# Third gate and up of the first expert loaded ahead of the short expert's, and returned rows loaded and added at the end, in a two-layer decoder trunk on one Trainium2 core

## The reference, cut to what matters

```python
def moe_swiglu(h, w_router, w_gate, w_up, w_down):
    t = h.reshape(B * S, D)
    logits = (t @ w_router).astype(jnp.float32)
    top_vals, top_idx = lax.top_k(logits, TOP_K)            # 2 of 8
    top_w = jax.nn.softmax(top_vals, axis=-1)
    gates = jnp.sum(jax.nn.one_hot(top_idx, N_EXPERTS) * top_w[..., None], axis=1)
    out = jnp.zeros_like(t)
    for e in range(N_EXPERTS):
        out = out + swiglu(t, w_gate[e], w_up[e], w_down[e]) * gates[:, e:e + 1]
    return out
# x = x + moe_swiglu(rms_norm(x)); return rms_norm(x, final_norm_g)
```

## Time and profile before

| | us |
|---|---|
| median of 3 runs | 1373.53 (1372.58 to 1374.31) |
| the profiled execution, its own time | 1372.62 |
| its span, first to last instruction | 1370.8 |
| PE busy | 1327.7 (97%) |
| DVE busy | 787.6 (57%) |
| ACT busy | 658.8 (48%) |
| POOL busy | 41.1 (3%) |
| first short expert's matmul begins | 558.6 |

### The profile page before, as it was taken

The page is one execution under the profiler, slowest core; times in us unless marked ns, Lnnn a source line. Parts: engine busy times, 40 slices in busy tenths (PEclk is TensorE's granted clock), DMA queues, the critical chain, the costliest instruction groups (busy, mean ns, idle before and its releaser), DMA issues.

```text
span 1370.8 us, 16922 instructions
## 1 busy us (share of the span) xinstructions
PE 1327.7 (97%) x6365; PEld 947.2 (69%) x6365; DVE 787.6 (57%) x912; ACT 658.8 (48%) x823; POOL 41.1 (3%) x45
## 2 busy tenths in 40 slices
PE   9999999999999999999999999899998999989997
PEld 8888788888888878755666556566555666646562
DVE  6556355555569757855565466464445565545561
ACT  5444445443464756554554455454445455444451
POOL 1000001000000010100000000000000000000000
PEclk9999999999999999999999999999999999999999
DMA  9745545555456437999999999999999999999994
GB/s 385 297 158 177 183 170 184 184 185 184 157 187 226 168 121 304 390 423 426 411 427 428 429 426 427 413 427 428 426 427 427 414 427 426 427 428 428 427 427 170
DMA packets 40448, 451.63 MB, mean 329 GB/s; under 512 B 4873, under 2 KB 5001, under 8 KB 8368
## 3 DMA queue, kind: packets, MB, share of 16 engines
q1 hardware_dynamic: 37408, 440.82, 79.0%
q0 software_dynamic: 2816, 9.63, 1.8%
q10 hardware_dynamic: 144, 0.09, 0.0%
HBM read 445.52 MB, written 6.55 MB: 330 GB/s over the span
## 4 chain that ended last, share of the span: by engine, by line
PE 79%; DMA 15%; DVE 3%; ACT 1%; issue 1%; POOL 0%; SPq 0%; DVEq 0%; ACTq 0%
PE psum L1939 18%; PE psum L1941 18%; PE psum L1940 18%; PE psum L2327 16%; DMA raw<-in_moe_w_gu 8%; DMA raw_more<-in_moe_w_gu 7%; PE psum L1985 1%; PE psum L1987 1%; PE psum L1986 1%; PE psum L1995 1%; DVE w_lo L1356 1%; ACT w_hi L993 1%; PE psum L2365 1%; PE psum L2358 1%; PE psum L2017 1%
## 5 line engine op out<-in xcount | busy, mean ns | idle before, releaser
L1356 DVE TENSOR_TENSOR w_lo<-raw,w_hi 128x1024 fp32r<-128x1024 f32 (+1 forms) x152 | 267.3, 1771 | 214.4 <-ACT w_hi L993 213.4
L993 ACT CAST w_hi<-raw 128x1024 fp32r<-128x1024 f32 (+1 forms) x152 | 225.3, 1492 | 226.2 <-PE psum L1941 150.2
L1941 PE MATMUL psum<-w_hi,actA_lo 128*128 128x512 f32 (+1 forms) x752 | 292.2, 389 | 0.0
L1939 PE MATMUL psum<-w_hi,actA_hi 128*128 128x512 f32 (+1 forms) x644 | 258.1, 401 | 25.2 <-DVE w_lo L1356 24.0
L1940 PE MATMUL psum<-w_lo,actA_hi 128*128 128x512 f32 (+1 forms) x644 | 250.0, 388 | 0.0
L1939 PEld LDWEIGHTS psum<-w_hi,actA_hi 128*128 128x128 f32 x644 | 122.2, 190 | 70.2 <-DVE w_lo L1356 35.8
L1941 PEld LDWEIGHTS psum<-w_hi,actA_lo 128*128 128x128 f32 x752 | 142.7, 190 | 30.1
L1356 DVE TENSOR_TENSOR w_lo<-raw_more,w_hi 128x1024 fp32r<-128x1024 f32 x76 | 91.2, 1223 | 102.1 <-ACT w_hi L993 101.8
L1940 PEld LDWEIGHTS psum<-w_lo,actA_hi 128*128 128x128 f32 x644 | 122.7, 190 | 22.0
L2327 PE MATMUL psum<-raw,const 128*64 128x512 f32 x608 | 134.7, 595 | 0.0
L993 ACT CAST w_hi<-raw_more 128x1024 fp32r<-128x1024 f32 x76 | 78.2, 1050 | 107.0 <-DMA raw_more<-in_moe_w_gu 70.6
(11 more groups left out here) (272 smaller groups left out, 1883.7 us busy)
## 6 DMA issues: line engine op xcount, KB each, us to landing
raw<-in_moe_w_gu SPq DMA_DIRECT2D x49, 2048.0 KB, 24.7
raw_more<-in_moe_w_gu SPq DMA_DIRECT2D x47, 2048.0 KB, 26.0
raw_more<-in_moe_w_down SPq DMA_DIRECT2D x24, 2048.0 KB, 26.2
raw<-in_moe_w_down SPq DMA_DIRECT2D x23, 2048.0 KB, 26.0
work<-in_moe_w_gu SPq DMA_DIRECT2D x16, 2048.0 KB, 26.2
raw<-in_ret_w_in SPq DMA_DIRECT2D x22, 1024.0 KB, 10.1
work<-in_moe_w_down SPq DMA_DIRECT2D x8, 2048.0 KB, 24.5
raw<-in_ffn_w_gate SPq DMA_DIRECT2D x11, 1024.0 KB, 4.8
```

What stands on the lines that cost most here:

```text
L993: nc.scalar.copy(hi_of(u)[:, 0:size], raw_of(w, u)[:, 0:size]).then_inc(sem["hi_ready"], 1)
L1356: nc.vector.tensor_tensor(lo_of(u)[:, 0:size], raw_of(w, u)[:, 0:size], as_f32(hi_of(u)[:, 0:size]), ALU.subtract).then_inc(sem["lo_ready" ...
L1939: nc.tensor.matmul(dst, l_hi[:, k, cols], r_hi[:, kk, rcols], start=first, stop=False)
L1941: return nc.tensor.matmul(dst, l_lo[:, k, cols], r_hi[:, kk, rcols], start=False, stop=last)
```

## The change

Two things are changed.

First, `FIRST` now has gate and up of the long expert's step 2 as blocks 5 and 6. They don't depend on the routing and stand ahead of the wait for `ranked`. Gate and up of the short expert's step 0 become blocks 7 and 8, behind that wait, and step 2's own two long blocks drop out of `load_pair(0)`. `block_of` and PE's `short_hidden("first", 0, FIRST_BLOCKS)` follow. In `free`, the next blocks for slots 5 and 6 (12 and 13) now wait for splits of the long expert's step 2, and those for slots 0 and 1 (14 and 15) for the short matmuls.

Second, POOL's read of `y_back` also waits until the short expert's down of step 5 has landed, the last block but the two halves. DVE's four additions of those rows move from the heads of steps 5 and 6 to a place behind the last `short_product`, just ahead of `combined`.

```diff
@@ block_of
             step, r = divmod(u - first_loop_unit, STEP_PARTS)
+            if w.base == 0 and step == 0 and r < KC:
+                return FIRST_BLOCKS - 2 + r // 4
             return FIRST_BLOCKS + STEP_BLOCKS * step + r // 4
@@ free
                 back = j - EXPERT_RAW
-                if back < 0 and w.base == 0:
-                    v = FIRST_BLOCKS + back
-                    if v < 5:
-                        long_split(n_dense + 4 * v + 3)
-                    else:
-                        sp.wait_ge(sem["pe_done"], w.pe("first", "short_gu", 0, v - 5))
+                v = FIRST_BLOCKS + back
+                if w.base == 0 and v < 5:
+                    long_split(n_dense + 4 * v + 3)
+                    return
+                if w.base == 0 and v < FIRST_BLOCKS:
+                    long_split(first_loop_unit + 4 * (v - 5) + 3)
+                    return
+                if w.base == 0 and v < FIRST_BLOCKS + 2:
+                    sp.wait_ge(sem["pe_done"], w.pe("first", "short_gu", 0, v - FIRST_BLOCKS))
                     return
@@ sync
-            FIRST = [("gu", 0, 0, 0), ("gu", 0, 0, 1), ("gu", 0, 1, 0), ("gu", 0, 1, 1), ("down", 0, 0, 0), ("gu", 1, 0, 0), ("gu", 1, 0, 1)]
+            FIRST = [("gu", 0, 0, 0), ("gu", 0, 0, 1), ("gu", 0, 1, 0), ("gu", 0, 1, 1), ("down", 0, 0, 0), ("gu", 0, 2, 0), ("gu", 0, 2, 1)]
...
-            for v in range(5):
+            for v in range(FIRST_BLOCKS):
                 first_free(v)
                 load(v, FIRST[v][0], None, *FIRST[v][2:], False)
             sp.wait_ge(sem["ranked"], 1)
...
-            for v in range(5, FIRST_BLOCKS):
-                first_free(v)
-                load(v, FIRST[v][0], short_first, *FIRST[v][2:], False)
+            for half in range(2):
+                long_split(n_dense + 4 * half + 3)
+                load(FIRST_BLOCKS + half, "gu", short_first, 0, half, False)
             load_pair(0)
@@ gpsimd
             pool.wait_ge(sem["y_done"], w.at("y_done", 16 * 4))
+            v = FIRST_BLOCKS + END_DOWN + 6
+            pool.wait_ge(sem["two_in"][v % EXPERT_RAW], w.block_in(v))
             pool.sem_inc(sem["back_asked"], 1)
@@ vector, expert_step
-                if n >= STEPS - 2 and at == "last":
-                    k = n - STEPS + 2
-                    for t in range(TILES):
-                        dve.wait_ge(sem["y_in"], 16)
-                        if k:
-                            dve.wait_ge(sem["comb"], t + 1)
-                        nc.vector.tensor_tensor(x[:, t, :], x[:, t, :], y_back[:, t, k, :], ALU.add).then_inc(sem["comb"], 1)
@@ vector, end
             short_product("last", STEPS - 1)
+            dve.wait_ge(sem["y_in"], 16)
+            for k in range(2):
+                for t in range(TILES):
+                    if k:
+                        dve.wait_ge(sem["comb"], t + 1)
+                    nc.vector.tensor_tensor(x[:, t, :], x[:, t, :], y_back[:, t, k, :], ALU.add).then_inc(sem["comb"], 1)
             dve.wait_ge(sem["comb"], 4)
             combined(("last", "combine"))
@@ tensor, first_steps
-                short_hidden("first", 0, 5)
+                short_hidden("first", 0, FIRST_BLOCKS)
```

More of the change, by code:

```diff
@@ L843, in load_pair @@
                 for n in range(2, STEPS + 2):
-                    j = load_blocks("pair", j, step_blocks(n), now, then, seen)
+                    done = 2 if base == 0 and n == 2 else 0
+                    j = load_blocks("pair", j + done, step_blocks(n)[done:], now, then, seen)
             for u, (src, kk, n) in enumerate(dense_sources):
```

## The result

The changed kernel takes 1375.28 us (median, 1373.84 to 1378.36); the kernel before, beside it, 1373.04. The ratio is 1.0017, 95% interval 1.001 to 1.0024: **2.2 us more**, a slowdown that can be told from zero but stays inside the 0.2% bound of the prediction. The forecast was 1376.0, no change by a hair. The profiled execution has a span of 1373.5 us against 1370.8, +2.7.

A forecast was written before the change was run, and what follows sets the result against it. DMA engines, never resting in the expert stage, were taken as the bound. Late slots +6.0 and rows -4.9 shift weights +1.1; the rows at the end make it +2.4, about 1376.0 us on the median's scale, range 1373.2 to 1379.6.

The forecast's parts named there:

- The win of the early loads: First loads: blocks 5 and 6 start 8.1 us sooner, but the queue is empty by block 11, so 0 gained.
- Rival 4: First loads and rows: the 8.1 us are kept as well, weights -13.0, total -11.7, 1361.8 us; chance 0.03.
- The cost of the late slots: Slots 5 and 6: blocks 12 and 13 wait for step 2's splits, DMA engines 6.0 us behind; bounds 5.4 and 6.9.
- ledger: Sum of block landings: idle-queue block 7.6 us, queued blocks 4.9 each; block 17 at 601.6, rows at 1359.5.
- Rival 3: Slots 5 and 6: late slots cost nothing because the queue refills from the stock; -3.6, 1369.9 us; chance 0.07.
- The rows out of the stage: Expert stage: the returned rows' 2048 KB leave the saturated DMA stage, -4.9 us for all weights behind it.
- The -0.6: Step 6: PE's 0.61 us wait for the split behind DVE's two additions goes, -0.6 us on PE's chain.
- The end: Last blocks: rows at 1359.5 plus four additions start `combined` at 1364.3, behind PE's chain (+0.5), setting the end at +2.4.
- the price of the transfer: Rows' read at the end: 7.6 us alone, like an SP block, issued at 1349.8, so 1357.4 alone, 1359.5 with sharing.
- Rival 1: End: rows land late, at 1362.3, sharing a full queue; `combined` +5.2, 1378.8 us, up to 1379.6; chance 0.17.
- Rival 2: End: rows come as if alone by 1357.4, PE's chain sets the end; +0.5, 1374.0 us; chance 0.13.

The follow-up runs named there:

- the rows alone: Kernel before plus only the later read of the returned rows and their additions at the end, old order of loads: 1370.12 us, ratio 0.9975.
- the additions alone: Kernel before with only the four additions moved to the end, the rows read as early as before: 1372.38 us, ratio 0.9997.
- the rows sooner, the sooner read: Kernel before with the later rows' read and additions at the end, old loads, but POOL waiting for the block two blocks earlier: 1369.21 us, ratio 0.9970.
- the exchanged slots: Changed kernel with ring slots 5, 6 and 0, 1 exchanged from block 12 on: 1369.55 us, ratio 0.9975 to the kernel before.
- the early loads alone: Kernel before with only the reordered first loads and their slot waits, returned rows read and added as before: 1380.90 us, ratio 1.0055.
- the rows behind everything: Changed kernel with POOL's read of the rows waiting for the very last half: 1380.92 us; the same issued by SP: 1380.01 us.
- +4: Changed kernel with exchanged slots, and POOL's read of the rows waiting for a block two blocks earlier than +6: 1367.37 us, ratio 0.9960.
- the rows in the weights' own queue: Changed kernel with SP issuing the rows directly behind the last half, with no wait for a landed block: 1378.03 us, ratio 1.0037.

## Why the prediction was right, step by step

**The win of the early loads, taken as 0: right.** Block 5 came 8.2 us sooner behind block 4 (forecast 8.1), block 11 at the same time. One reason given holds only for the trace it was read from: there block 10 had landed (555.7) when block 11 was issued, so that the queue was empty at this point already before the change; in the rows alone, the additions alone and the rows sooner, which all keep the old loads, block 10 lands 1.3 to 1.6 us after that issue. The changed kernel has it landed in time again (555.7), but with the exchanged slots block 17 comes no sooner behind block 11 than in those three (below). Rival 4 falls all the same, and the exchanged slots show the same from the other side: early loads without late slots are worth nothing that can be measured.

**The cost of the late slots, 6.0 us: right, with some luck.** Block 12 at 568.79 and 13 at 574.34 (forecast 568.9 and 574.4), an empty queue from 564 to 568; block 17 at 602.4 for 601.6, so 6.8, inside the bounds of 5.4 and 6.9. The ledger is 0.8 short by block 13's landing, 8.1 us where I took the 7.6 of an idle queue, and by four blocks at 5.0 rather than 4.9. That half alone gave 7.4 at block 17 and 7.1 as its time, just above the bounds.

But the 595.6 that all this is measured against is early. From the issue of block 11 to the landing of block 17 the trace of before has 39.5 us. The three other kernels with the old loads have 41.1 (rows alone), 41.0 (additions alone) and 40.7 (rows sooner), the two with the exchanged slots 40.8 and 41.5, the six with the late slots 46.4 to 47.1. By these the late slots cost 5.3 to 6.4 us. Block 17 in the additions alone, and a stretch of the kernel before and then of the additions alone (third last column: granted clock):

```profile
L814 SPq DMA_DIRECT2D raw<-in_moe_w_gu x1: 333/333/333, 587.4 to 587.4; - x1
DMA to landing us min/median/max: 9.6/9.6/9.6
...
520.00:525.00 5.00, 5.00 (x30) 5.00 (x31) 3.32 (x10) 1.72 (x3) 0.00 (x0) 0.67 0.26 59
...
520.00:525.00 5.00, 4.96 (x41) 4.55 (x42) 4.67 (x15) 2.38 (x4) 0.61 (x1) 1.00 0.00 0
```

In the trace of before the granted clock stood at 0.50 (1.2 GHz) from about 520 to 523.5 us, behind a wait of PE of 0.4 us at 518 (the additions alone have the same wait and no such fall), and block 11 came 1.6 us later behind block 4 than in those three kernels, which gave the queue time to catch up. So two errors of about a microsecond cancel in the 6.0: a start that was too early, and a ledger that was short. Rival 3, the late slots cost nothing, was priced at 1369.9; the run that removed their cause gave 1369.55.

**The rows out of the stage, -4.9: right.** 4.7 at the last half with that part alone, and PE's idle time from 1160 to 1300 fell by 4.4. The -0.6 for the additions that leave step 6 is shown as far as PE's wait goes: 0.61 us before and 0.58 in the early loads alone, the two kernels that have the additions there, and no such wait in any of the ten others. As a time it isn't shown, and the forecast of +2.4 doesn't contain it, since the rows set the end. How much PE's chain gains differs, too: from its matmuls at 1308 to its last group it is 48.4 us in the changed kernel, 0.9 less than before, but 50.0 in the rows alone, where the granted clock stood at 0.50 (1.2 GHz) from 1304 to 1307 us, behind a wait of PE of 2.1 us; the changed kernel has that wait too (2.2 us), without the fall.

**The end, +2.4: right in size, for a reason that was half wrong.** `combined` at 1364.55 for 1364.3, the rows at 1359.8 for 1359.5, PE's chain +0.5 as forecast. But I had argued from a queue "still full at 1349.6". It wasn't. Stretches of the changed kernel, with POOL's request at 1350.49:

```profile
1346.00:1348.00 2.00, 2.00 (x12) 0.72 (x10) 0.00 (x0) 0.00 (x0) 0.00 (x0) 1.00 0.65 274
1348.00:1350.00 2.00, 2.00 (x12) 0.65 (x10) 0.00 (x0) 0.00 (x0) 0.00 (x0) 1.00 0.51 213
1350.00:1352.00 2.00, 2.00 (x12) 0.64 (x10) 0.00 (x0) 0.14 (x1) 0.77 (x1) 1.00 0.45 176
```

With two halves still to land, half the DMA engines' time is free. And the halves weren't slowed by the rows: the last one lands 4.9 us behind block +6, as before. The step that failed is the price of the transfer. I had 7.6 for it alone, from an SP block, and let the sharing fill the rest; in fact it takes 9.3 here and 9.4 alone, so nearly all of it is its own price, and POOL's issue comes 0.6 us behind the landing, not 0.2. The ledger's 1359.5 is right for rows that really stand in the queue (1359.1 when SP queued them); that POOL's transfer lands at the same time is chance. The error would have shown in any variant with another number of blocks beside it: it made the run with the rows behind everything come out about 2 us above what I expected.

**Rivals 1 and 2** lived off the same price. Rival 2 (rows as if alone, PE's chain sets the end, 1374.0) needed the rows at 1357.4; they came 2.4 us later, 0.7 by POOL's issue (1350.49 for 1349.8) and 1.7 by the transfer. The lower end of the range, 1373.2, is given for this rival at the lower cost, which its own line puts at 1373.4; nothing hangs on it. Rival 1 (the rows shared with weights for long) didn't come here, but with two blocks more in the queue it did: 16.6 us. The rule that I quoted from the Trainium skill (DMA: Bandwidth & Descriptors, Rules for kernel authors), to issue early and wait late, agrees with these runs only within the last blocks: there POOL's request put sooner made the time shorter, from 1380.92 (behind all) to 1375.28 (behind +6) in the changed kernel, and from 1369.55 (+6) to 1367.37 (+4) with the exchanged slots. Over the whole program it does not: the kernel before asks for the rows at 1195.9 us, earliest of all, and asking for them behind +6 made it 3.65 us faster, because their bytes no longer stand among the weights.

## What to carry to other kernels

In a ring that one queue fills in order, a load moved ahead was worth nothing that could be measured here, as the next slots didn't come free sooner, and it costs if the block that now sits in that slot is used up later: after reordering loads, compare the order in which slots are *emptied* with the order in which they are *asked for*. What the loss costs showed here some 200 us later as idle time of an engine that was never starved at the place of the edit, so look for it in the DMA share there, not in waits. Moving a transfer out of a saturated stage was worth its bytes (4.7 us for 2048 KB), but at the end it has to be requested so early that its whole time from issue to landing, for the queue that issues it, lies beside other work, and its bytes may make the last weights late: in the sooner read PE waited for them twice. And one trace of before can be off by a microsecond in just the stretch that a ledger starts from; the traces of kernels that do the same there tell.

## What the hardware showed that was not expected

A read of 2048 KB from DRAM took 9.4 us from issue to landing when POOL issued it on idle DMA engines, and 7.6 us when SP issued the very same one. Stretches of the two kernels that read the rows behind everything, at the start and the end of the transfer, POOL's first (issued at 1356.70), then SP's (issued at 1355.09). A packet counts in the stretch in which it starts, so a short stretch can show a share above 1:

```profile
1357.80:1358.00 0.20, 0.00 (x0) 0.00 (x0) 0.16 (x1) 0.00 (x0) 0.00 (x0) 1.00 0.00 0
1358.00:1358.20 0.20, 0.19 (x2) 0.19 (x4) 0.00 (x0) 0.00 (x0) 0.00 (x0) 1.00 0.34 41
...
1364.00:1365.00 1.00, 0.44 (x4) 0.00 (x0) 0.00 (x0) 0.00 (x0) 0.00 (x0) 1.00 0.06 25
1365.00:1365.50 0.50, 0.00 (x0) 0.00 (x0) 0.00 (x0) 0.00 (x0) 0.00 (x0) 1.00 0.08 33
```

```profile
1355.50:1356.00 0.50, 0.50 (x4) 0.14 (x2) 0.00 (x0) 0.00 (x0) 0.00 (x0) 1.00 0.00 0
1356.00:1356.20 0.20, 0.20 (x4) 0.11 (x2) 0.00 (x0) 0.00 (x0) 0.00 (x0) 1.00 2.94 328
...
1362.00:1362.40 0.40, 0.28 (x2) 0.00 (x0) 0.00 (x0) 0.07 (x1) 0.00 (x0) 1.00 0.01 0
```

POOL's transfer moves nothing in the 1.3 us up to 1358.0, SP's nothing in the 0.9 us up to 1356.0, and both start within the next 0.2 us. So some 0.4 us of the 1.8 lie ahead of the first byte. Most of the rest lies at the end: SP's bytes are through at 1362, while POOL's transfer goes on until 1365.5 at 25 to 33 GB/s, a share of 0.06 to 0.08, which is the time of about one of the 16 engines. Why, no run here shows.

The second thing: the DMA share of a queue that ends falls, in the kernel before, from 0.91 (1342 to 1344 us) over 0.56 (1346 to 1348) to 0.12 (1352 to 1354), while halves still have to land. Rows that SP queues behind them fill that room, in the kernel with the rows in the weights' own queue:

```profile
1346.00:1348.00 2.00, 2.00 (x12) 0.59 (x10) 0.00 (x0) 0.00 (x0) 0.00 (x0) 1.00 0.89 377
```

But it didn't make them land sooner: the share then falls in the same way at the rows' own end, over 0.62 (1350 to 1352) to 0.22 (1356 to 1358), and they land a block's time, 4.9 us, behind the last half.
